# Two more places for expert weights, handed out in order of freeing, in a two-block model on one core

## The chip, the core and the metric

The kernel runs on one core of a Trainium2 chip. The metric is the device time of one execution in microseconds, the median of several runs. All data is float32; TensorE takes some operands as fp32r (a float32 written so that TensorE reads it in fewer passes). The engines are TensorE (PE), VectorE (DVE), ScalarE (ACT), GpSimd (POOL) and SyncE (SP); each works its own queue in order, and they meet by semaphores. SyncE issues nearly all weight loads.

## The reference, cut to what matters

Two blocks follow each other. The first has two layers of a hybrid mixer over 256 tokens of width 1024. The second puts 16 meta tokens ahead (272 rows in all) and has two layers, each a mixer and then a mixture of experts:

```python
def hier_moe(h, w_grp, b_grp, w_rtr, b_rtr, w1, w3, w2):
    grp_prob = softmax(t @ w_grp + b_grp)                 # 4 groups
    g_prob, g_sel = top_k(grp_prob, 1)
    exp_logits = (t @ w_rtr + b_rtr)                      # 32 experts, 8 a group
    e_prob, e_sel = top_k(softmax(in_grp), 2)             # 2 of the 8
    hid = silu(t @ w1[e]) * (t @ w3[e])                   # 1024 -> 256, for each expert e
    y = sum over e of (hid * combine[e]) @ w2[e]          # 256 -> 1024
for l in range(2):
    mix = concat(deltanet_group(...), dsa_group(...)) @ w_out[l]
    h = layer_norm(ALPHA * h + mix, ...)
    h = layer_norm(ALPHA * h + hier_moe(h, ...), ...)
```

The weights of all 32 experts are read in each of the two layers: w1 and w3 take 2 MB an expert, w2 takes 1 MB, 96 MB a layer.

## The kernel before

**The loads.** SyncE walks through one list of loads from first to last (`load`, L620 in the trace). Each load is 1 MB, 128 partitions by 2048 float32, and goes into a place ("slot") of that size. The class `Ring` works out, ahead of time, for each load its place, the count at which it has landed, and the semaphore and value that say that the last user of that place is done. SyncE waits for that value and then issues; so a load whose place isn't free holds back all loads behind it.

**The places.** Slots 0 to 5 are a ring of their own, used by all mixers in turn. In an expert stage more places are taken from tiles that are dead by then: three in `projT` (slots 6 to 8), two in the arena (`ONCE`, slots 9 and 10), one in `prm` and one more in `projT` (`LASTING`, 11 and 12). That makes 13. The list `places` starts with two ring slots, both arena slots, the three in projT, the four other ring slots, the two lasting ones; behind that a cycle of 12 repeats, the same without slot 10. SyncE waits for `delta_over` ahead of load 2 (arena is free), `room_free` ahead of load 4 (projT is free) and `layer_normed` ahead of load 11 (prm is free).

**The order of expert loads** (`moe_order`): the four "up" loads of pair 0, then for each pair its four up loads followed by the two "down" loads of the pair before. 16 pairs, 96 loads a layer. A stage is that of one layer.

**TensorE in a stage** (`experts_grouped`): `gather_pair` (L1719) picks the rows of the first pairs, `up_half(i, 0)` and `up_half(i, 1)` (L1668, 16 products of 512 columns each) wait for two loads each and count `up_used`; between them stand `turn` (L1677), `add_up` of the pair before last (L1758, adds the pair's rows into the group's sum) and small selections; then `gather_two` (L1737) and `down(i - 1)` (L1695, 16 products) on two loads. In the loads' order each of these blocks frees two places.

**ScalarE and VectorE in a stage.** ScalarE copies gathered rows (`tokens_in`, L2223), makes the sigmoid (`gate_sigmoid`, L2242 and on) and copies the high part of the down product's rows, half by half (`rows_high_out`, L2255). VectorE follows with the low part (`rows_out`, L2922). In the second half VectorE counts `down_used` once ScalarE's copy is done: that gives the two down places back (L2920).

**POOL in a stage.** It stores the normed rows to memory (L3042), gathers the rows of each of four groups by index (L3049, into `xrows`), sends the sums of the groups back by index (L3014) and reads them at the end (L3057).
**Around.** `cosT`, `sinT` (tables of the first block), `posi` (positions) and `xselT` (a selection written by ScalarE at pair 10 and read at the end of the stage) have tiles of their own. Behind the first stage comes the next layer's mixer, whose first six w_in loads go into the ring slots 3, 4, 5, 0, 1, 2.

## Time and profile before

| | us |
|---|---|
| median of 3 runs | 1416.46 |
| lowest and highest | 1414.64, 1419.3 |
| the profiled execution, its own time | 1419.17 |
| its span, first to last instruction | 1417.4 |
| TensorE busy | 1321.5 (93%) |
| VectorE busy | 572.6 (40%) |
| ScalarE busy | 487.4 (34%) |
| POOL busy | 47.2 (3%) |
| moved by the DMA engines | 306.14 MB, mean 216 GB/s |
| granted TensorE clock, mean | 0.982 |

How to read it: the first block takes the span up to about 350 us, the second block's first layer up to some 885 us with its expert stage from about 640 us on, the second layer the rest with its stage from about 1167 us on. In the view of stretches the columns are: from and to, its length, then busy us (and number of instructions) of PE, PEld (the weight loads of TensorE), DVE, ACT and POOL, the granted TensorE clock as a share, the busy share of the 16 DMA engines, and GB/s. In the chain of waits a line "issue" is time in which the engine waited for nothing that an engine or a recorded event explains; a wait for a transfer that had its landing unnoticed can stand there too. In the timeline, what stands in brackets is the idle time ahead and who ended it.

### The profile page before, as it was taken

What the parts mean: (1) busy time and instruction counts of PE and PEld (TensorE: products, weight loads), DVE (VectorE), ACT (ScalarE), POOL (GpSimd) and SP (SyncE); (2) the same over time, 40 slices, a digit from 0 to 9 for tenths busy, and PEclk for the clock granted to TensorE, in tenths of its full rate; (3) what the DMA queues carried; (4) which work ended last, traced back from release to release, by engine and by line L of the source; (5) the groups of instructions that cost most, each with busy time, mean ns of one, the idle gap of its engine ahead of it and who ended that gap; (6) DMA issues with size and microseconds to landing.
All of it is one profiled execution on the core that took longest, in us unless ns stands there. A gap on an engine that the chain in (4) does not pass through costs nothing. (4 is left out here: it accounts for less than half of the span.)

```text
span 1417.4 us, 18978 instructions
## 1 busy us (share of the span) xinstructions
PE 1321.5 (93%) x7405; PEld 845.7 (60%) x7405; DVE 572.6 (40%) x1240; ACT 487.4 (34%) x1065; POOL 47.2 (3%) x68
## 2 busy tenths in 40 slices
PE   6999989999999999989999978999998999999886
PEld 5778567784788877554344432688776654344332
DVE  2235213252577384351222214578485342222214
ACT  3245332462562234312223222473124412223222
POOL 0000000000001000000000000002000000000000
PEclk9999999999999999999999999999999999999999
DMA  8553152331521132556999999131132557999993
GB/s 343 121 148 117 60 211 89 120 119 35 208 93 58 60 126 83 208 212 237 422 420 421 422 417 381 65 110 71 60 120 90 208 215 296 420 422 422 422 423 163
DMA packets 48670, 306.14 MB, mean 216 GB/s; under 512 B 5849, under 2 KB 6361, under 8 KB 17216
## 3 DMA queue, kind: packets, MB, share of 16 engines
q1 hardware_dynamic: 43584, 285.47, 50.8%
q0 software_dynamic: 3808, 10.32, 3.0%
q10 hardware_dynamic: 1184, 9.05, 1.7%
q8 instruction: 64, 1.05, 0.3%
q14 instruction: 30, 0.25, 0.0%
HBM read 299.81 MB, written 8.59 MB: 218 GB/s over the span
## 5 line engine op out<-in xcount | busy, mean ns | idle before, releaser
L1035 PE MATMUL ps<-hT,ring 128*128 128x272 f32 (+1 forms) x1984 | 473.8, 394 | 7.0 <-ACT projT L1884 3.1
L1035 PEld LDWEIGHTS ps<-hT,ring 128*128 128x128 f32 x1984 | 375.4, 193 | 82.5 <-issue 13.3
L1668 PE MATMUL ps<-projT,arena 128*64 128x512 f32 x496 | 167.2, 596 | 7.7 <-issue 6.3
L1668 PE MATMUL ps<-ring,arena 128*64 128x512 f32 x384 | 168.1, 601 | 3.5 <-issue 3.5
L1695 PE MATMUL ps<-ring,arena 128*64 128x512 f32 x384 | 119.8, 607 | 12.3 <-issue 12.3
L1668 PEld LDWEIGHTS ps<-projT,arena 128*64 128x64 f32 x496 | 49.8, 137 | 101.1 <-issue 100.7
L2922 DVE TENSOR_TENSOR xo<-ps,xo 128x512 fp32r<-128x512 f32 x64 | 43.0, 690 | 115.4 <-ACT xo L2255 115.4
L1695 PEld LDWEIGHTS ps<-ring,arena 128*64 128x64 f32 x384 | 35.0, 138 | 78.5 <-issue 76.7
L2911 DVE TENSOR_TENSOR arena<-arena,ps 128x256 f32<-128x256 f32 x32 | 13.5, 422 | 157.7 <-ACT arena L2244 157.3
L1993 ACT ACTIVATE projT<-ps 128x272 f32<-128x272 f32 x68 | 27.0, 398 | 144.1 <-PE ps L1035 142.7
L1668 PEld LDWEIGHTS ps<-ring,arena 128*64 128x64 f32 x384 | 46.8, 137 | 32.8 <-issue 31.5
L2242 ACT ACTIVATE arena<-ps 128x256 f32<-128x256 f32 x32 | 12.3, 385 | 138.8 <-PE ps L1668 133.8
L1286 PE MATMUL ps<-ring,projT 128*128 128x512 f32 x128 | 56.6, 596 | 0.0
L2255 ACT ACTIVATE xo<-ps 128x512 fp32r<-128x512 f32 x64 | 36.7, 598 | 56.5 <-PE ps L1695 56.5
L1075 PE MATMUL ps<-ring,arena 128*128 128x512 f32 x128 | 55.9, 593 | 0.0
L1884 ACT ACTIVATE projT<-ps 128x256 f32<-128x256 f32 x56 | 21.5, 384 | 95.7 <-PE ps L1035 94.2
L1695 PE MATMUL ps<-arena 128*64 128x512 f32 x112 | 54.2, 629 | 0.0
L1668 PE MATMUL ps<-prm,arena 128*64 128x512 f32 x112 | 51.1, 598 | 0.0
L2223 ACT ACTIVATE arena<-ps 128x1024 f32<-128x1024 f32 x28 | 28.5, 1016 | 50.5 <-PE ps L1737 50.5
L2248 ACT ACTIVATE arena<-ps 128x256 f32<-128x256 f32 x32 | 12.3, 384 | 89.3 <-PE ps L1677 89.3
L1758 PE MATMUL ps<-xo,pselT 128*128 128x512 f32 x128 | 38.7, 419 | 3.0 <-DVE xo L2922 3.0
L1075 PEld LDWEIGHTS ps<-ring,arena 128*128 128x128 f32 x128 | 24.1, 190 | 28.4 <-issue 28.2
(485 smaller groups left out, 1787.4 us busy)
## 6 DMA issues: line engine op xcount, KB each, us to landing
ring<-experts SPq DMA_DIRECT2D x96, 1024.0 KB, 18.2
ring<-w_in SPq DMA_DIRECT2D x62, 1024.0 KB, 4.9
projT<-experts SPq DMA_DIRECT2D x62, 1024.0 KB, 18.3
arena<-experts SPq DMA_DIRECT2D x18, 1024.0 KB, 16.2
ring<-w_out SPq DMA_DIRECT2D x16, 1024.0 KB, 4.8
prm<-experts SPq DMA_DIRECT2D x16, 1024.0 KB, 20.9
prm<-params ACTq DMA_DIRECT2D x2, 2048.0 KB, 7.8
prm<-params ACTq DMA_DIRECT2D x2, 1152.0 KB, 10.2
```

The costliest lines, as they stand in the source:

```text
L1035: mm = pe.matmul(ps[:, 5 + j % banks, 0:ncols], w[:, j % 2, k, :], hT[:, k, T - ncols:T], start=(k == 0), stop=(k == KC - 1))
L1075: return pe.matmul(ps[:, (0, 5)[t - 1] + half, :], yT[:, 2 * GROUP_ORDER[i] + c, c0:c0 + P], w[:, c, 512 * half:512 * half + 512], start=( ...
L1286: mm = pe.matmul(ps[:, (4 if t == 1 else 2) + h, :], rows(pair, c), weights(i)[:, c, 512 * h:512 * h + 512], start=first, stop=last)
L1668: mm = pe.matmul(ps[64 * e:64 * e + 64, 0, :], xg[:, 4 * h + k, i % 2, 64 * e:64 * e + 64], w[e][:, k // 2, 512 * (k % 2):512 * (k % 2) + ...
L1695: mm = pe.matmul(ps[64 * e:64 * e + 64, 4 + half, :], xhT[:, f, 64 * e:64 * e + 64], w[e][:, f, 512 * half:512 * half + 512], start=(f == ...
L1758: mm = pe.matmul(ps[:, 6 + half, :], pselT[:, q, :], xo[:, part, 512 * half:512 * half + 512], start=(q == 0 and part == 0), stop=(q == PA ...
L1884: L(a.activation(projT[:, j, META:T], ps[:, 5 + j % 2, 0:SEQ], ACT.Copy), s("projection_copied"))
L1993: L(a.activation(projT[:, j, :], ps[:, 5 + j % 2, 0:T], ACT.Copy), s("projection_copied"))
L2223: a.activation(xg[:, 4 * half:4 * half + 4].rearrange("p (b k) c n -> p b (k c n)", b=2), ps[:, 2:4, :], ACT.Copy)\
L2255: a.activation(xo[:, 0, 512 * half:512 * half + 512], ps[:, 4 + half, :], ACT.Copy)\
L2911: VP(v.tensor_tensor(xh, xe, ps[:, 0, 0:256], ALU.mult))
L2922: v.tensor_tensor(low, ps[:, 4 + half, :], high, ALU.subtract).then_inc(s("pair_rows_copied"), 1)
```

## The change

- **Two more places.** `SPARE` (slot 13) is a new tile of 1 MB. `LENT` (slot 14) is another, in which `cosT`, `sinT`, `xselT` and `posi` now live; it is used for expert loads only up to load 57 of a stage, before `xselT` is written. The space comes from the tables that are now inside it and from the scratch of POOL's transfers, 4096 instead of 16384 bytes a partition.
- **The order.** `free` is a queue: each load takes its head and goes to its end, so places come round in the order in which their loads are used up. Ahead of a load a place whose last use is past (`LAST_USE`: LENT 57, the second arena slot 75) is dropped. The first 15 loads go to SPARE, ring, LENT, ring, both arena slots, three in projT, four ring slots, two lasting ones. Worked out, LENT is last used by load 47, the second arena slot by load 64. The waits for `delta_over`, `room_free` and `layer_normed` stand ahead of loads 4, 6 and 13.
- **ScalarE gives down weights back.** `down_used` is counted by ScalarE when TensorE's second half is done, ahead of its own copy of that half, and no longer by VectorE behind ScalarE's copy.
- **Moved.** The arena's `yacc` (used only in a branch that this input doesn't take) and `xrows` change places, so that the two arena slots stay clear; `group_tokens` gets a tile of its own. At the start two semaphores become one and one is dropped for another that counts the same instructions.

```diff
-ALL_SLOTS = 13
+SPARE, LENT = 13, 14
+ALL_SLOTS = 15
+
+LAST_USE = {LENT: 57, ONCE[1]: 75}
...
-                    rest = [*range(SLOTS, SLOTS + MORE_SLOTS), *own[2:], *LASTING]
-                    places = own[0:2] + list(ONCE) + rest
-                    cycle = own[0:2] + list(ONCE[:1]) + rest
-                    while len(places) < len(moe_order()):
-                        places += cycle
+                    free = [SPARE, own[0], LENT, own[1], *ONCE, *range(SLOTS, SLOTS + MORE_SLOTS),
+                            *own[2:], *LASTING]
+                    places = []
+                    for j in range(ITEMS_MOE):
+                        while j > LAST_USE.get(free[0], ITEMS_MOE):
+                            free.pop(0)
+                        places.append(free.pop(0))
+                        free.append(places[-1])
...
-        cosT = sb("cosT", SEQ)[:, :]
-        sinT = sb("sinT", SEQ)[:, :]
+        spare = sb("spare", SLOT)
+        lent_at = -(-nc.sbuf_base // 32) * 32
+        lent = sb("lent", SLOT)
+        assert nc.sbuf_base == lent_at + 4 * SLOT
+        cosT, sinT = lent[:, 0:SEQ], lent[:, SEQ:2 * SEQ]
+        xselT = lent[:, 2 * SEQ:2 * SEQ + T]
+        posi = nc.alloc_sbuf_tensor_at("posi", [P, SEQ], I32, offset=lent_at + 4 * (SLOT - SEQ))
+        rows_high = ctx.enter_context(nc.sbuf_tensor("rows_high", [P, D], F32R))[:, :]
...
+            if slot in (SPARE, LENT):
+                return (spare if slot == SPARE else lent)[:, :]
...
-                    if j == 2:
+                    if j == 4:
...
-                    if j == 2 + len(ONCE):
+                    if j == 6:
...
-                    if j == 2 + len(ONCE) + MORE_SLOTS + ITEMS_WO:
+                    if j == 6 + MORE_SLOTS + ITEMS_WO:
...
-        xrows, ax = more(ax, D)
         rows_low = halved("rows_low", ax, D)[:, :]
         ax += D
+        xrows, ax = more(ax, D)
...
-        group_tokens = posi[:, 0:GROUPS]
+        group_tokens = ctx.enter_context(nc.sbuf_tensor("group_tokens", [P, GROUPS], I32))[:, :]
...
                             a.wait_ge(s("pair_down_done"), 2 * i + half + 1)
+                            if half == 1:
+                                a.sem_inc(down_used, 1)
...
                         v.wait_ge(s("pair_rows_high"), 2 * i + half + 1)
-                        if half == 1:
-                            v.sem_inc(down_used, 1)
...
-    nc = bacc.Bacc("TRN2", target_bir_lowering=False, num_devices=1)
+    nc = bacc.Bacc("TRN2", target_bir_lowering=False, num_devices=1, dynamic_dma_scratch_size=4096)
```

## Rows read from the trace of the kernel before

**Rows 1.** The page's 40 equal slices: DMA busy tenths, GB/s.
```profile
DMA  8553152331521132556999999131132557999993
GB/s 343 121 148 117 60 211 89 120 119 35 208 93 58 60 126 83 208 212 237 422 420 421 422 417 381 65 110 71 60 120 90 208 215 296 420 422 422 422 423 163
```

**Rows 2.** Busy by stretch: us, busy us (instructions) per engine, PEclk, DMA, GB/s.
```profile
790.00:872.00 82.00, 70.04 (x319) 28.32 (x316) 16.64 (x27) 19.36 (x37) 2.69 (x4) 0.98 1.01 419
...
1301.00:1397.30 96.30, 83.81 (x390) 35.25 (x391) 20.36 (x37) 24.05 (x46) 3.17 (x4) 0.98 0.97 403
```

**Rows 3.** The same view, stretches of the DMA stream.
```profile
600.00:605.00 5.00, 5.00 (x13) 2.19 (x12) 3.10 (x6) 0.00 (x0) 0.00 (x0) 1.00 0.00 0
646.10:675.00 28.90, 28.27 (x148) 13.27 (x150) 7.13 (x15) 7.39 (x14) 0.00 (x0) 1.00 0.83 316
675.00:870.00 195.00, 183.73 (x876) 75.87 (x873) 45.17 (x87) 52.32 (x99) 7.77 (x9) 0.99 1.01 421
850.00:855.00 5.00, 3.83 (x11) 1.28 (x13) 0.00 (x0) 0.23 (x1) 0.00 (x0) 0.66 1.01 424
1172.60:1205.00 32.40, 31.77 (x169) 15.02 (x170) 8.35 (x19) 8.70 (x17) 1.01 (x1) 1.00 0.84 326
```

**Rows 4.** The page: POOL's DMA queue, and expert loads into the ring.
```profile
q0 software_dynamic: 3808, 10.32, 3.0%
...
ring<-experts SPq DMA_DIRECT2D x96, 1024.0 KB, 18.2
```

**Rows 5.** Chain of waits, second expert stage: start us, us, what.
```profile
1160.17 6.69 DMA arena<-normed_rows,posi
...
1184.25 3.58 PE ps L1668 x16
...
1193.69 3.58 PE ps L1668 x16
...
1198.93 3.58 PE ps L1668 x16
...
1247.81 3.58 PE ps L1668 x16
...
1373.22 3.34 issue
1376.56 5.35 PE ps L1695 x16
```

**Rows 6.** Timeline of TensorE behind the first expert stage: start us, us, what.
```profile
875.54 0.73 PE L1758 MATMUL ps<-xo,pselT 128*128 128x512 f32 x2
...
896.84 3.48 PE L1035 MATMUL ps<-hT,ring 128*128 128x272 f32 x14 [0.75 <-ACT hT L1859]
```

**Rows 7.** Timeline of SyncE's queue: start us, us over all, what, count.
```profile
646.07 0.81 SPq L620 DMA_DIRECT2D ring<-experts  x2
...
847.55 29.00 SPq L620 DMA_DIRECT2D ring<-w_in  x6
...
1172.64 0.81 SPq L620 DMA_DIRECT2D ring<-experts  x2
1177.22 0.33 SPq L620 DMA_DIRECT2D arena<-experts  x1
1183.47 4.73 SPq L620 DMA_DIRECT2D projT<-experts  x3
```

**Rows 8.** Line L620, the issues at 1172.6 and at 1208.2.
```profile
DMA to landing us min/median/max: 4.8/4.8/4.8
...
DMA to landing us min/median/max: 12.4/12.4/12.4
```

**Rows 9.** Timeline of ScalarE and VectorE: row copies of pair 0, second stage.
```profile
1194.65 1.08 ACT L2255 ACTIVATE xo<-ps 128x512 fp32r<-128x512 f32 x2
...
1195.27 1.29 DVE L2922 TENSOR_TENSOR xo<-ps,xo 128x512 fp32r<-128x512 f32 x2 [5.04 <-ACT xo L2255]
```

**Rows 10.** Line L3049, the gathers of rows: ns min/median/max.
```profile
L3049 POOL DMA_INDIRECT arena<-normed_rows,posi x8: 1009/1020/1085, 634.8 to 1310.2; - x8
```

More of the change, by code:

```diff
@@ L397, in program @@
         assert nc.sbuf_base == arena_at + 4 * AR
-        posi = ctx.enter_context(nc.sbuf_tensor("posi", [P, SEQ], I32))
-        rows_high = ctx.enter_context(nc.sbuf_tensor("rows_high", [P, D], F32R))[:, :]
         ps = ctx.enter_context(nc.psum_tensor("ps", [P, 8, 512], F32))
@@ L444, in program @@
         start_in = sem("start_in")
-        start_head = sem("start_head")
         x_in = [sem("x_in_1"), sem("x_in_2")]
@@ L458, in program @@
         rows_fetched = sem("rows_fetched")
-        seen = sem("seen")
         layer_seen = sem("layer_seen")
@@ L628, in _ @@
             head = CONSTS["few"][1]
-            sp.dma_start(cst[:, 0:head], A["consts"][:, 0:head]).then_inc(start_head, 16)
+            sp.dma_start(cst[:, 0:head], A["consts"][:, 0:head]).then_inc(start_in, 16)
             for t in (1, 2):
@@ L730, in program @@
         room = 3 * LG
-        yacc, ad = more(room, KC, T)
-        hid, ad = more(ad, 2, T)
+        hid, ad = more(room, 2, T)
         e1b, ad = more(ad, 2, T)
         cbb, ad = more(ad, T)
+        yacc, ad = more(room + 2 * D, KC, T)
         combT, ad = more(ad, T)
@@ L739, in program @@
         downw, ad = more(ad, SLOT)
+        assert ad <= AR - 2 * D
         rtmp, _ = more(ONCE_AT + len(ONCE) * SLOT, T)
@@ L1844, in _ @@
                 LT(a.activation(hT[:, k, META:T], ps[:, k % 4, 0:SEQ], ACT.Copy, scale=g_first[:, k:k + 1]), head_act)
-            a.wait_ge(seen, 1)
+            a.wait_ge(tables_vec, 16)
             L0(a.activation(sinT, sinT, ACT.Sin))
@@ L2303, in _ @@
             V0(v.memset(sg[:, 0, :], 0.0))
-            v.wait_ge(start_in, 16)
-            v.wait_ge(start_head, 16)
+            v.wait_ge(start_in, 32)
             V0(v.tensor_copy(cosT, posi[:, :]))
@@ L2316, in _ @@
             V0(v.tensor_tensor(cosT, cosT, arena[:, 4 * D:4 * D + SEQ], ALU.add))
-            V0(v.tensor_scalar(cosT, cosT, 3.1415925, -3.1415925, ALU.min, ALU.max), seen)
+            V0(v.tensor_scalar(cosT, cosT, 3.1415925, -3.1415925, ALU.min, ALU.max))
             for t in (1, 2):
```

1 line of the change is left out of this document (removed).

## The prediction

> **What bounds the kernel now.** I read the 40 slices of the page first [rows 1]. Twice, for some 200 us, the DMA line stands at 9 and the rate at 420 GB/s: those are the two expert stages, one per layer of the second block. TensorE is busy 70.0 of the last 82 us of the first stage and 83.8 of the last 96.3 us of the second [rows 2]: 12.0 and 12.5 us of waits, while before that it is busy without a break. In the chain of waits they appear as "issue" in front of L1668 and L1695, the products on expert weights, where no engine had anything left to do for them, 3.34 us the longest [rows 5]. The long stretches of the DMA engines [rows 3] show why: a stage needs 96 loads of 1 MB [rows 4], and at 421 GB/s one takes 1.0486 MB / 0.421 = 2.49 us, so the six of a pair of experts take 14.9 us. TensorE's own pace is shorter: in the chain of waits the first L1668 block of a pair stands at 1193.69 and that of the fourth pair after it at 1247.81; 54.1 us, 13.5 us a pair [rows 5]. So TensorE runs on the stock laid in before, uses it up by 790 us (1301 us in the second stage) and then follows the stream. Behind the longest wait the block takes 5.35 us and not 3.58 [rows 5]; at the same place of the first stage the granted clock is 0.66 over 5 us [rows 3], a mix of the 1.2 and the 2.4 GHz level, after an idle TensorE. The end of a stage is set by when the 94th load lands, that is by (a) how many loads are in before TensorE starts and (b) how long the DMA engines stand idle after that.
>
> As to (b): the stream opens when TensorE hands back its first places, at 646.07 us and at 1172.64 us [rows 7]. From there to 675 us it moves 316 GB/s and from 1172.6 to 1205 us 326 GB/s, against 421 afterwards [rows 3]. So 28.9 x (1 - 316/421) = 7.2 us and 32.4 x (1 - 326/421) = 7.3 us are lost in each opening. The cause is in the old order of places. The second place in the arena is used once only, so that from then on a load waits for a product later than the oldest one finished: SyncE issues one load at 1177.22 and stands till 1183.47 [rows 7].
>
> **Two more places.** 15 loads instead of 13 are in before the stage begins; 81 are left instead of 83. That is 2 x 2.49 = 5.0 us off the stream in each stage. The cost ahead: two more issues on SyncE (0.33 us for the single one [rows 7]) and 5.0 us more of transfers at about 569 and 1105 us. They are hidden: the DMA engines move nothing in 600:605 [rows 3], while all early places are full, and the loads that run beside the stores and the gather of rows at the head of the stage, four into the last ring places and two into the lasting ones, stay these six. If that cover were gone it would be up to 5.0 us a stage.
>
> **Places in order of freeing.** I walk through the second stage with SyncE's issues [rows 7] and the ends of TensorE's blocks in the chain [rows 5], two places handed back at each, 4.8 us from issue to landing on an idle queue [rows 8] and 2.49 us a load on a busy one. Returns at 1172.6, 1177.2, 1183.4, 1187.8, then at 1195.2 the down weights of pair 0 (by ScalarE, [rows 9]), then 1197.3 and 1202.5. Landings: 1177.4, 1179.9; 1182.4, 1184.9; 1188.2, 1190.7; 1193.2, 1195.7; 1200.0, 1202.5; a gather of 0.5 MB of rows by POOL comes in between, 1.2 us; 1206.2, 1208.7; 1211.2. Holes left: 0.8 us before the third pair of loads, 1.8 us before the fifth, and the first lead of 4.8 - 2.5 = 2.3 us, together 4.9 us. By bytes the opening thus loses 4.9 instead of 7.3 us, gain 2.4, with the two loads **7.4 us**. By landings it is more: the 28th load (index 27), one into the arena, was issued at 1208.2 and landed 12.4 us later, at 1220.6 [rows 8]; in my walk it lands at 1211.2, **9.4 us** earlier. Since the byte count takes every stretch between loads at the full rate and the landing count has a walk without any friction, I take the middle, 8.4 us. The first stage has the same pattern with nearly the same loss, so the same value.
>
> **ScalarE gives down weights back.** VectorE did it on its second row copy, which follows ScalarE's copy. For pair 0 ScalarE's two copies take 1194.65 to 1195.73, the second starting near 1195.2; VectorE's two differences take 1195.27 to 1196.56, the second starting near 1195.9 [rows 9]. So the hand-back comes 0.6 to 0.7 us earlier. It is of worth only where a hole stands behind it, in front of the fifth pair of loads: 0.6 us a stage, and it is already in the walk. With 81 loads that wait on the rate alone it is nothing elsewhere. The price is one semaphore instruction in ScalarE's queue ahead of the copy of the second half, 32 in all; queued behind it are that copy, VectorE's difference and the L1758 product. No row times such an instruction; the nearest is SyncE's issue of one transfer, 0.33 us [rows 7]. Only the last pair of each stage has nothing over it, and the same instruction goes from VectorE, which is next in that chain: between 2 x 0.33 us lost and 2 x 0.33 us gained. I take 0, the two being one for one.
>
> **Smaller DMA scratch.** 16384 to 4096 bytes concern POOL's transfers alone. Their queue has 3808 packets in the whole run, 238 per DMA engine [rows 4]. One of them stands on TensorE's chain at the head of each stage, the gather of rows, which took 6.69 us from issue to landing [rows 5]; the store of the rows ahead of it is of the same kind. What a smaller scratch costs no row shows. Bounds: nothing, or the landing time of the gather once more for each of the two, 13.4 us a stage. Below nothing I exclude: the transfers stay the same. I take nothing, because none of the eight gathers took over 1.085 us to issue [rows 10].
>
> The Trainium skill ("SBUF — State Buffer", SBUF size) gives the carve-out as 16 KiB, and its DMA page ("DMA: Bandwidth & Descriptors", The descriptor swizzle) counts 9 descriptors a side and engine for 1 MB; at 16 bytes each that would leave room for many such transfers in 4 KiB, which goes with nothing. No run here shows it.
>
> **The rest.** Merged start semaphores, moved tiles, a token table of its own, the swap of two row buffers: same instructions, same sizes, 0 us; the cover is not needed. The lent place leaves after load 57 and the second arena place after 75; by then loads land 18.2 us after issue in the median [rows 4] and the rate alone counts, 0 us. Behind the first stage six w_in loads are issued from 847.55 to 876.5 us, and their first product starts at 896.84 [rows 6, 7]. Now the third of them waits for the last down product; the row copies behind that one end by 875.5 us [rows 6], so it is free by 867.1 us, and 4.8 and 3 x 2.5 us more give 879.4 us, ahead of 896.84 - 8.4 = 888.4 us. 0 us.
>
> **Sum.** 2 x 8.4 = 16.8 us. What is late next: still the stream. TensorE could give back at most 12.0 + 12.5 us of waits and 2 x 1.8 us of the slow blocks, 28.1 us, so some 10 us of waits stay. The profiled execution took 1419.17 us (span 1417.4), giving 1402.4; the median of the runs shown is 2.7 us lower, 1416.46, and gives **1399.7 us**.
>
> The Trainium skill ("DMA: Bandwidth & Descriptors", Specifications) names 435 GB/s as the fabric's ceiling and about 358 GB/s as HBM's limit for a core. The trace's 421 GB/s agrees with the first and contradicts the second; by 358 a load would take 2.93 us and two of them would be worth 5.9 and not 5.0 us a stage.
>
> **The rivals.**
> Only the stock counts (chance 0.20). The holes stay, because in the opening the places come back no faster than TensorE's blocks end, whatever the order. For it: two holes remain even in my walk. Against: the one-load issue at 1177.22 goes away. 2 x 5.0 = 10 us, 1406.5, from 1404 to 1408.5.
> TensorE becomes the bound (0.07). The stream comes over 11 us earlier in each stage, if the holes left in my walk (0.8 + 1.8 us) close too. 21 to 28 us, 1388.5 to 1395.5.
> The extra stock does not stand ready, or the time is given back behind the stage (0.07): the spare loads sit in SyncE's queue behind the ring's places, and the gain melts to within 4 us. Against: nothing moves in 600:605 [rows 3], so the stock of early places is complete 40 us ahead of the stage.
> Slower (0.05): POOL's transfers wait for descriptor room. Mechanism: store and gather at the head of a stage are in TensorE's chain [rows 5]; each made longer by the gather's 6.69 us costs 13.4 us a stage, 26.8 us, less 16.8: 1426.5. It decides from 8.4 us more a stage. Against: the packets per engine above.
> The forecast has 0.58, with 1397 to 1402.5 as its own range; 0.03 lie elsewhere. A measurement of this kernel tells about 0.3%, 4.2 us, from no change. The range 1394.5 to 1407.5 takes in the forecast, most of "only the stock" and the nearer part of the TensorE case, and leaves out 0.19. Faster by more than 0.3%: 0.58 + 0.20 + 0.07 + 0.03 = 0.88; within: 0.07; slower: 0.05.
>
> **What would show it.** Right: SyncE's issues in the opening come in twos (1172.6, 1177.2, 1183.4, 1187.8), the rate from the opening on stays near 400 GB/s, TensorE's waits in the last 90 us fall from 12 to about 4 or 5 us a stage, the 3.3 us wait shrinks or goes. Wrong: the opening still at 320 GB/s (only the stock), no waits left (TensorE the bound), a longer wait before the first L1719 block (POOL), or first w_in products that wait.

## The result and the profile after

The changed kernel takes 1401.97 us in the median of four runs (1399.52 to 1404.07) and the kernel before, timed beside it, 1416.91 (1414.64 to 1419.3): ratio 0.9894, interval 0.987 to 0.9918, 14.9 us less. The profiled execution took 1402.93 us, span 1401.1. Timed once more later, the changed kernel took 1400.84 us against 1418.47: ratio 0.9874, interval 0.9854 to 0.9893. The ratios leave out two slow executions, one of 1724.14 us of the kernel with late end reads and one of 4678.78 us of the kernel before beside it. In the code everything from L620 on has moved down by eight lines or so: L620 is now L628, L1668 is L1676, L1695 is L1703, L3057 is L3064.

The DMA and GB/s lines of the page, in 40 slices, for [rows 1]:

```profile
DMA  8553252321531133556999998131132657999993
GB/s 352 117 148 110 72 214 90 121 101 50 187 119 62 61 121 120 241 207 261 419 420 421 422 417 343 68 118 63 61 120 84 277 218 289 422 421 422 421 421 141
```

The two plateaus have the same height, 421 GB/s, and the slices behind them have less left to move: 343 for 381 and 141 for 163. The megabytes in all are the same, 306.14.

The stretches, columns as in [rows 2, 3]: both openings, the last 82 and 96 us of the stages, and 5 us each around the longest wait:

```profile
641.70:670.60 28.90, 28.27 (x148) 13.30 (x150) 7.13 (x15) 7.39 (x14) 0.00 (x0) 1.00 0.95 379
776.50:858.50 82.00, 78.11 (x365) 31.11 (x365) 19.19 (x35) 21.67 (x42) 3.69 (x5) 0.98 1.01 416
842.00:847.00 5.00, 4.47 (x14) 1.79 (x16) 0.00 (x0) 0.00 (x0) 0.00 (x0) 0.66 1.02 429
1163.00:1195.40 32.40, 31.77 (x168) 14.95 (x170) 8.35 (x19) 8.69 (x17) 1.01 (x1) 1.00 0.95 371
1285.00:1381.00 96.00, 90.19 (x422) 36.53 (x418) 21.29 (x39) 26.27 (x50) 3.17 (x4) 0.96 0.95 396
1359.50:1364.50 5.00, 4.42 (x12) 1.51 (x14) 0.07 (x1) 0.60 (x1) 0.00 (x0) 0.50 1.02 428
```

The openings moved 316 and 326 GB/s before [rows 3] and move 379 and 371 now. TensorE waited 12.0 and 12.5 us at the end of a stage before [rows 2]; now 82 - 78.11 = 3.9 and 96 - 90.19 = 5.8 us.

SyncE's queue in the second opening, for [rows 7]:

```profile
1162.97 0.33 SPq L628 DMA_DIRECT2D spare<-experts  x1
1163.35 0.43 SPq L628 DMA_DIRECT2D ring<-experts  x1
1167.54 0.33 SPq L628 DMA_DIRECT2D lent<-experts  x1
1167.91 1.20 SPq L628 DMA_DIRECT2D ring<-experts  x1
1173.79 0.80 SPq L628 DMA_DIRECT2D arena<-experts  x2
```

Two loads go out at each hand-back, at 1163.0, 1167.5 and 1173.8 us, where the old order had one at 1177.22 and then stood until 1183.47 [rows 7].

The chain of waits, the longest waits of both stages and what follows them, for [rows 5]:

```profile
813.03 27.16 DMA ring<-experts
840.18 2.34 issue
842.53 5.35 PE ps L1676 x16
...
1328.91 28.78 DMA projT<-experts
1357.69 2.39 issue
1360.08 6.28 PE ps L1703 x16
```

In the chain the waits are 2.3 to 2.4 us, but in the second stage it counts as "issue" only what comes after a landing at 1357.69. TensorE's timeline has the whole idle time in brackets:

```profile
842.53 2.24 PE L1676 MATMUL ps<-ring,arena 128*64 128x512 f32 x6 [2.41 <-issue]
```

```profile
1360.08 1.09 PE L1703 MATMUL ps<-projT,arena 128*64 128x512 f32 x1 [3.71 <-issue]
```

Measured in this way, the longest wait of a stage was 3.6 and 3.3 us before, is 2.4 and 3.7 us here, and 3.9 and 3.1 us in the second execution of the changed kernel. So it has not shrunk; what went are most of the waits of about 1.2 us around it. The block behind each long wait still runs partly at the 1.2 GHz level (granted clock 0.66 and 0.50 over 5 us, in the stretches above) and takes 5.35 and 6.28 us; in TensorE's timeline a block at full clock takes 3.65.

**The length of a stage.** I take it from the start of its first up block to the start of its last down block. For the first stage these are the first of the two following lines of TensorE's timeline in the kernel before, and the second in the changed kernel, whose own first up block starts at 637.68:

```profile
641.92 4.10 PE L1668 MATMUL ps<-ring,arena 128*64 128x512 f32 x16
```

```profile
858.36 3.65 PE L1703 MATMUL ps<-ring,arena 128*64 128x512 f32 x16
```

Before, the last down block starts at 871.84 (stage 229.92 us); after, 858.37 - 637.68 = 220.69. The second stage: 1168.95 to 1397.22, 228.27 us, against 1159.27 to 1380.95, 221.68. Together 458.19 and 442.37: **15.8 us less**. All that lies outside the stages is 1417.4 - 458.19 = 959.2 us before and 1401.1 - 442.37 = 958.7 after. The part behind the last down block of the second stage, called the tail below, is 20.15 us before and 20.18 after. The other parts shift by 4 us against each other (ahead of the first stage 641.92 and 637.68, between the stages 297.1 and 300.9), while the stretches at the lower clock level lie elsewhere in each execution: the granted clock between the stages is 0.98 before and 0.96 after. The same kernel run again has 639.3 and 297.5, and 0.98 between the stages. I compare stages, therefore, and not absolute times.

### The profile page after: what moved, and what is told of

It is laid out like the page before. It is cut to its first block, busy times and chain, and to the rows that moved or that the text cites. A ratio compares the mean times of both kernels' runs of the same rounds, so it can differ in the third digit from the quotient of the medians.

```text
span 1401.1 us, 18978 instructions
## 1 busy us (share of the span) xinstructions
PE 1322.1 (94%) x7405; PEld 845.5 (60%) x7405; DVE 572.5 (41%) x1240; ACT 486.9 (35%) x1065; POOL 47.2 (3%) x68
## 2 busy tenths in 40 slices
DMA packets 48414, 306.14 MB, mean 218 GB/s; under 512 B 5849, under 2 KB 6361, under 8 KB 16704
## 4 chain that ended last, share of the span: by engine, by line
PE 76%; DVE 11%; DMA 6%; ACT 5%; issue 2%; POOL 0%; SPq 0%; DVEq 0%; ACTq 0%; POOLq 0%
PE ps L1043 24%; PE ps L1676 14%; PE ps L1703 7%; PE ps L1294 4%; PE ps L1083 4%; DMA projT<-experts 2%; PE ps L1745 2%; DMA ring<-experts 2%; PE ps L1766 2%; PE ps L1051 1%; PE ps L1513 1%; DVE projT L2578 1%; DVE small L2577 1%; PE ps L1519 1%; DMA normed_rows<-res 1%
## 5 line engine op out<-in xcount | busy, mean ns | idle before, releaser
L1043 PEld LDWEIGHTS ps<-hT,ring 128*128 128x128 f32 x1984 | 375.1, 192 | 82.4 <-issue 13.4
L1676 PE MATMUL ps<-ring,arena 128*64 128x512 f32 x416 | 140.4, 607 | 3.4 <-issue 3.4
L1676 PEld LDWEIGHTS ps<-ring,arena 128*64 128x64 f32 x416 | 40.8, 139 | 65.5 <-issue 64.5
L1676 PE MATMUL ps<-projT,arena 128*64 128x512 f32 x272 | 80.0, 597 | 0.0
L1703 PE MATMUL ps<-ring,arena 128*64 128x512 f32 x224 | 72.8, 597 | 0.0
L1703 PE MATMUL ps<-projT,arena 128*64 128x512 f32 x160 | 68.1, 615 | 4.7 <-issue 4.7
L1676 PE MATMUL ps<-arena 128*64 128x512 f32 x144 | 50.9, 597 | 1.2 <-ACT arena L2235 1.2
L1676 PE MATMUL ps<-prm,arena 128*64 128x512 f32 x96 | 43.7, 598 | 0.0
L1294 PEld LDWEIGHTS ps<-ring,projT 128*128 128x128 f32 x128 | 23.8, 190 | 28.0 <-issue 28.0
## 6 DMA issues: line engine op xcount, KB each, us to landing
ring<-experts SPq DMA_DIRECT2D x80, 1024.0 KB, 16.8
projT<-experts SPq DMA_DIRECT2D x54, 1024.0 KB, 17.6
```

Source lines behind the costliest of these rows:

```text
L1043: mm = pe.matmul(ps[:, 5 + j % banks, 0:ncols], w[:, j % 2, k, :], hT[:, k, T - ncols:T], start=(k == 0), stop=(k == KC - 1))
L1294: mm = pe.matmul(ps[:, (4 if t == 1 else 2) + h, :], rows(pair, c), weights(i)[:, c, 512 * h:512 * h + 512], start=first, stop=last)
L1676: mm = pe.matmul(ps[64 * e:64 * e + 64, 0, :], xg[:, 4 * h + k, i % 2, 64 * e:64 * e + 64], w[e][:, k // 2, 512 * (k % 2):512 * (k % 2) + ...
L1703: mm = pe.matmul(ps[64 * e:64 * e + 64, 4 + half, :], xhT[:, f, 64 * e:64 * e + 64], w[e][:, f, 512 * half:512 * half + 512], start=(f == ...
```

## The experiments

Every run below has a profile. "Stages" are the two lengths and their sum as above, "rest" is the span without them.

| kernel | stages | sum | rest | median us | ratio, interval |
|---|---|---|---|---|---|
| before | 229.92, 228.27 | 458.19 | 959.2 | 1416.91 | |
| changed | 220.69, 221.68 | 442.37 | 958.7 | 1401.97 | 0.9894, 0.987 to 0.9918 |
| changed, again | 222.91, 219.63 | 442.54 | 957.1 | 1400.84 | 0.9874, 0.9854 to 0.9893 |
| 15 places, old order | 223.45, 221.43 | 444.88 | 959.3 | 1405.56 | 0.9912, 0.9887 to 0.9937 |
| 13 places, new order | 227.17, 226.57 | 453.74 | 961.2 | 1415.4 | 0.9966, 0.9937 to 0.9996 |
| VectorE gives back | 222.81, 221.52 | 444.33 | 962.2 | 1406.34 | 0.9895, 0.9852 to 0.9937 |
| ScalarE gives back, alone | 228.80, 226.56 | 455.36 | 957.5 | 1418.58 | 1.0012, 0.999 to 1.0034 |
| small scratch, alone | 229.89, 228.30 | 458.19 | 963.0 | 1417.75 | 0.9991, 0.997 to 1.0012 |
| 14 places | 223.77, 222.79 | 446.56 | 958.6 | 1409.36 | 0.9945, 0.9923 to 0.9968 |
| half loads | 215.01, 213.39 | 428.40 | 959.4 | 1389.73 (one) | |
| late end reads | 218.10, 218.42 | 436.52 | 966.8 | 1412.22 | 0.9952, 0.9921 to 0.9984 |
| late end reads, added last | 219.02, 217.83 | 436.85 | 960.2 | 1402.18 | 0.9902, 0.9873 to 0.993 |
| reads after the last up weights | 219.07, 218.48 | 437.55 | 975.4 | 1409.99 | 0.9932, 0.9905 to 0.9958 |
| the same, added last | 218.74, 216.93 | 435.67 | 964.5 | 1404.64 | 0.99, 0.9872 to 0.9928 |

**15 places in the old order.** The fixed cycle comes back, ScalarE still gives back:

```
-                    places = []
-                    for j in range(ITEMS_MOE):
-                        while j > LAST_USE.get(free[0], ITEMS_MOE):
-                            free.pop(0)
-                        places.append(free.pop(0))
-                        free.append(places[-1])
+                    places, cycle = list(free), [x for x in free if x != ONCE[1]]
+                    while len(places) < ITEMS_MOE:
+                        places += [x for k, x in enumerate(cycle) if len(places) + k <= LAST_USE.get(x, ITEMS_MOE)]
```

> 15 places as in the changed kernel, but from load 15 on handed out in the old fixed cycle, in which the second arena place does not come again; ScalarE gives back. Theory 'stock plus order': the stock is worth 5.0 us a stage, ScalarE's hand-back 0.6; the cycle skips one place, so from load 20 on a load waits for the product after the right one, and SyncE issues a single load at the third hand-back. That keeps 2.4 us a stage of the old holes. Against the kernel before: 6 us a stage, 12 us in all, ratio 0.9915. Stage lengths (first up block to the last down block) 224 and 222 us against 229.9 and 228.3. Rival 'only the stock counts': the same time as the changed kernel, 15 us under before, ratio 0.989, stages 221 us.

Its stages are 2.5 us longer together than those of the changed kernel, near the 224 and 222 us expected. SyncE in the first opening, and the stretches of both:

```profile
656.75 0.33 SPq L625 DMA_DIRECT2D arena<-experts  x1
661.14 6.23 SPq L625 DMA_DIRECT2D projT<-experts  x3
```

```profile
645.90:674.80 28.90, 28.27 (x148) 13.32 (x150) 7.13 (x15) 7.38 (x14) 0.00 (x0) 1.00 0.88 335
1166.20:1198.60 32.40, 31.77 (x169) 15.02 (x170) 8.34 (x19) 8.69 (x17) 1.01 (x1) 1.00 0.90 352
```

The single issue is back, SyncE stands for 4 us behind it, and the rates are 335 and 352 GB/s against 379 and 371.

**13 places in order of freeing.**

```
-                    free = [SPARE, own[0], LENT, own[1], *ONCE, *range(SLOTS, SLOTS + MORE_SLOTS),
+                    free = [own[0], own[1], *ONCE, *range(SLOTS, SLOTS + MORE_SLOTS),
```

(and SyncE's three waits ahead of loads 2, 4 and 11, as before the change).

> The changed kernel with its two new places left unused: 13 places, handed out in the order of freeing, ScalarE gives back. Theory 'stock plus order': what is left is the closing of holes in the opening, 2.4 us a stage by bytes and 4.4 by landings, so 3.5 us a stage, 7 us under before, ratio 0.995; SyncE issues in twos from the first hand-back on. Rival 'only the stock counts': within 1 us of before.

The two openings:

```profile
645.80:674.70 28.90, 28.28 (x149) 13.26 (x150) 7.12 (x15) 7.38 (x14) 0.00 (x0) 1.00 0.95 355
1171.90:1204.30 32.40, 31.78 (x168) 14.92 (x170) 8.34 (x19) 8.69 (x17) 1.01 (x1) 1.00 0.96 373
```

The holes are mostly gone (DMA share 0.95 and 0.96 for 0.83 and 0.84 in [rows 3]), yet the stages are only 4.45 us shorter together, where 7 were expected. Two more places, on top of this, are worth 453.74 - 442.37 = 11.4 us.

**VectorE gives back**, as before, in an otherwise changed kernel.

```
-                            if half == 1:
-                                a.sem_inc(down_used, 1)
...
+                        if half == 1:
+                            v.sem_inc(down_used, 1)
```

> The changed kernel with one part undone: VectorE gives the down weights back behind ScalarE's copy. Theory: a load waits for it only at the fifth hand-back of each stage, 0.6 us later, so 0.6 us a stage, 1.2 us over the changed kernel (ratio to before 0.990). The issue behind the first down block comes 0.6 to 0.7 us later. Rival: ScalarE's part is worth nothing or costs something (its queue has one instruction more), then the stages are as long as in the changed kernel or shorter.

The stages are 2.1 us longer and 0.2 us shorter, one each way; the sum is 2.0 us longer, where 1.2 was expected.

**Small scratch alone**, in the kernel before: `dynamic_dma_scratch_size=4096`.

> The kernel before with the DMA scratch at 4096 bytes and nothing else. Theory: 0 us, ratio 1.000; store and gather of rows land after the same 8 and 3 to 7 us. Rival 'descriptor room': POOL's transfers in the chain ahead of each stage take longer, up to 13.4 us a stage, ratio up to 1.019.

The stages are 229.89 and 228.30 us against 229.92 and 228.27: no difference. The queue of POOL's transfers has the same packets as in [rows 4]:

```profile
q0 software_dynamic: 3808, 10.32, 2.9%
```

The ratio says the same, 0.9991 (0.997 to 1.0012).

**Half loads.** What is the floor? This kernel leaves out half of each expert load, so it shows times alone.

```
-                    load((kind, l, i, h, e), A["experts"][m * P:(m + 1) * P, :])
+                    load((kind, l, i, h, e), A["experts"][m * P:(m + 1) * P, :], 1)
...
-                                           w[e][:, k // 2, 512 * (k % 2):512 * (k % 2) + 512], ...
+                                           w[e][:, 0, 512 * (k % 2):512 * (k % 2) + 512], ...
...
-                                                w[e][:, f, 512 * half:512 * half + 512],
+                                                w[e][:, 0, 512 * half:512 * half + 512],
```

> The changed kernel, but each load of expert weights moves only its first half (0.5 MB instead of 1 MB), and TensorE reads that half in place of both. The products on expert weights thus use wrong weights, and half of the expert weights never come; the instructions of TensorE, their sizes and their order are the same. It shows how long a stage is when the stream no longer bounds it, and with that what is left to gain after the change. Theory 'the stream still sets the end of a stage': the changed kernel's stages (first up block to last down block) take 220.7 and 221.7 us; in their last 82 and 96 us TensorE waits 3.9 and 5.8 us, and about 1.8 us more are lost to one block at the lower clock level. So stages of about 215 us, no wait of over 0.5 us for a load in the chain, and a profiled time of about 1391 us (span 1389, give or take 4 us for stretches of lower clock outside the stages). Rival 'TensorE is already the bound and its own clock or VectorE and ScalarE make the waits': stages of 220 us and more, time within 3 us of 1402.

The last 82 and 96 us of its stages:

```profile
772.50:854.50 82.00, 81.33 (x393) 33.11 (x391) 19.97 (x37) 24.06 (x46) 3.69 (x5) 1.00 0.62 216
1272.00:1368.00 96.00, 95.04 (x460) 38.56 (x458) 23.81 (x43) 27.85 (x53) 4.18 (x5) 1.00 0.59 202
```

TensorE waits 0.7 and 1.0 us there, and the granted clock is 1.00. Its own work makes stages of 215.01 and 213.39 us, in all 14.0 us less than in the changed kernel and 29.8 us less than before. So the stream still sets the end of a stage after the change.

**ScalarE gives back, alone**, in the kernel before: the last edit the other way round.

> The kernel before, with one edit alone: ScalarE gives the down weights back in place of VectorE. The forecast gave 0.6 us a stage where a hole stands behind the fifth pair of loads, and nothing at the end of a stage. With it: 0 to 1.2 us less than the kernel before, 1416 us, stages of 229.3 and 227.7 us. The change without this edit had stages of 222.81 and 221.52 us against 220.69 and 221.68 with it, so a rival gives it 2 us in the first stage: 1414.5 us. Third, that it is worth something only once loads are placed in order of freeing (in the old order the load behind the hand-back waits for something later anyway): stages as in the kernel before, 229.9 and 228.3 us, within 0.3 us.

The stages are 1.1 and 1.7 us shorter, 2.8 us together; the median tells nothing (ratio 1.0012, 0.999 to 1.0034).

**14 places**, the spare one without the lent one.

> The changed kernel with one extra place instead of two (14 places: the spare one, not the lent one). By the stream's rate a place is worth one load, 2.49 us a stage. Theory 'a place is worth its bytes': between the kernel with 13 places in order of freeing (stages 227.17 and 226.57 us) and the changed kernel (220.69 and 221.68), so stages of 224 us each, whole time about 1408. Rival 'the first place does most of it, then TensorE's pace or the clock takes over': stages of 221.5 to 222.5 us, whole time about 1404. Rival 'the second does most, since only then the wait that turns the clock down is gone': stages of 226 us, whole time about 1412.

The sum, 446.56, stands between 453.74 (13 places) and 442.37 (15): 7.2 us for the first place and 4.2 for the second, 11.4 for both. The stages are near the 224 us expected of a place worth its bytes, but by this sum the first place is worth more than its 2 x 2.49 us and the second less. Why was not tried.

**The changed kernel once more.**

> The changed kernel itself once more, timed beside the one above. Both theories: 1402 us median within 3 us, ratio to the kernel before 0.986 to 0.993, stages of 221 and 222 us within 1 us. It tells how far a stage moves between executions of one kernel: if it is less than 0.5 us, the differences of 2 us between the single edits in the first stage are real; if it is 1.5 us or more, they are not.

This run put the others right. Its stages are 222.91 and 219.63 us where the first execution had 220.69 and 221.68: 2.2 us longer and 2.1 us shorter, with the same sum within 0.2. One stage of one profile can't carry a statement on 2 us, and the 2.1 us in the first stage of "VectorE gives back" are no more than that. Sums of both stages repeat far better in the two pairs on record: 442.37 and 442.54 here, 458.19 twice in the kernel before and the one with the small scratch.

**What makes one stage differ from the next.** Each load counts up its semaphore sixteen times, once by each DMA engine, and the trace has the time of each. For load 93 (counted from 0: the second down load of the last pair but one) I take the first and the last of the sixteen, both counted from SyncE's first issue of the opening. The down block of that pair waits for this load: it starts within 0.3 us of the last of the sixteen in the runs of this table, and the last down block, with which a stage ends, follows 5.8 to 6.1 us later:

| kernel | first engine, stages 1 and 2 | last engine |
|---|---|---|
| before | 212.3, 213.0 | 219.8, 218.7 |
| changed | 203.9, 205.2 | 210.6, 211.8 |
| changed, again | 204.2, 205.6 | 212.5, 209.7 |
| 15 places, old order | 206.6, 207.4 | 213.5, 211.6 |
| 13 places, new order | 209.6, 209.6 | 217.2, 216.7 |
| VectorE gives back | 207.9, 205.7 | 212.7, 211.9 |
| ScalarE gives back, alone | 212.0, 212.3 | 218.5, 216.7 |
| 14 places | 205.7, 206.7 | 213.6, 212.9 |

In the two executions of the changed kernel the first engine is done within 0.4 us of the same time. The last one, for which TensorE has to wait, is 1.9 us later in one stage and 2.1 us earlier in the other, and that is how much the stages differ. The spread from first to last is 2.0 us at load 27 and 6.7 us at load 93 of the first stage: the DMA engines drift apart while the queue is deep. With half loads, which land 4.3 and 4.7 us after issue at load 27, the spread at load 93 is 1.2 and 0.4 us. The Trainium skill ("DMA: Bandwidth & Descriptors", Why a DMA increments its semaphore by 16 and not by 1) says that the engines finish independently and that only the full 16 mean that the data is there. The trace agrees. What slows the late engine was not tried.

Between two executions of the changed kernel the first engine is the steadier measure, and by it the edits add up (mean of the two stages, us a stage): two places 209.6 - 204.6 = 5.0 in the new order and 212.2 - 207.0 = 5.2 in the old; the order 212.2 - 209.6 = 2.6 with 13 places and 207.0 - 204.6 = 2.4 with 15; ScalarE's hand-back 212.7 - 212.2 = 0.5. The 0.5 is hardly more than the 0.4 by which the measure itself moved. By the same measure VectorE's hand-back in the changed kernel costs 4.0 us in the first stage and 0.5 in the second. The second agrees with 0.5; the 4.0 stay unexplained, and the last engine is there within 0.2 us of the changed kernel's second execution (212.7 and 212.5). So the first engine too can mislead by some us.

TensorE waits for the last engine, and by that column the split is another: two places 5.8 (new order) and 5.1 (old), the order 0.7 (13 places) and 1.4 (15), ScalarE's hand-back 1.7. The lengths of the stages say the same. So the order makes most engines some 2.5 us earlier a stage and the late one, which counts, about 1. By the first engine the first extra place is worth 3.4 us and the second 1.6.

**Late end reads.** From the trace of the changed kernel: near 828 us and 1348 us POOL reads about 1.1 MB of sums back (L3064), in the middle of the last loads, though VectorE needs them only behind the last pair but one. Here POOL waits first:

```
                 g.wait_ge(sums_sent, 16 * SENT * (l + 1))
+                g.wait_ge(down_used, PAIRS * (l + 1) - 1)
```

> The changed kernel, with one wait more in POOL's queue: its three reads of the chosen rows at the end of a stage (about 1 MB, queued at some 829 us and 1349 us, in the middle of the last expert loads) wait until ScalarE has given back the down weights of the last pair but one. In the changed kernel loads 84 to 88 of the first stage land 3.7, 4.2 and 3.8 us apart instead of 2.5. Theory 'the reads take their bytes out of the stream ahead of the load that TensorE waits for': that load comes about 2.5 us earlier in each stage, the 2.4 us wait nearly goes, and with it the block at the lower clock level (1.8 us): stages of 216.5 to 219 us, whole time 4 to 8 us less than the changed kernel, 1394 to 1398 us. Rival 'the reads come too late': VectorE needs these rows for the sums that follow the stage, their landing takes 6 to 10 us, and the end of the stage waits for them: stages as in the changed kernel or shorter, but the time between the last down block and the next block's first product longer by 2 to 6 us, whole time 1400 to 1408. Third, 'hidden anyway': the load waited for is late because one DMA engine lags, not by bytes: 1402 within 1.5.

The end of the second stage in the chain of waits:

```profile
1357.48 1.38 issue
...
1362.51 1.31 issue
...
1372.38 1.27 issue
...
1378.46 4.54 DMA arena<-chosen
...
1383.02 1.24 DVE res L2944
...
1384.28 1.24 DVE res L2944
```

The wait of 3.7 us has become three of 1.3, the granted clock over the last 96 us is 1.00 for 0.96, and the stages are 5.9 us shorter together:

```profile
1283.00:1379.00 96.00, 90.92 (x438) 37.78 (x436) 21.87 (x40) 27.25 (x52) 4.15 (x5) 1.00 0.97 404
```

But behind the second stage VectorE waits 4.5 us for the reads and adds them, 2.5 us, in front of the last row difference: the tail grows from 20.18 to 23.60 us. Behind the first stage it is worse. VectorE waits 8.0 us for the reads there and TensorE 8.1 us for VectorE:

```profile
863.11 1.22 DVE L2944 SCALAR_TENSOR_TENSOR res<-res,hT 128x1024 f32<-128x1024 f32 x1 [7.97 <-DMA arena<-chosen]
```

```profile
867.62 2.07 PE L1766 MATMUL ps<-xo,pselT 128*128 128x512 f32 x4 [8.12 <-DVE xo L2929]
```

```profile
855.90:887.40 31.50, 20.80 (x78) 9.05 (x77) 19.06 (x27) 10.62 (x24) 0.06 (x1) 0.89 0.48 190
```

TensorE's clock falls behind that wait (0.89 over the stretch, 1.00 in the changed kernel). From the last down block to the first product on w_in it is 31.53 us where the changed kernel has 23.17: 8.4 us more, and with the 3.4 of the tail 11.8 us against the 5.9 gained. The rival "too late" holds.

**Late end reads, added last.** VectorE adds the rows behind its last copies:

```
-                    chosen_added(VP)
                     rows_out(PAIRS - 1)
                     sums_in(GROUPS - 1)
+                    chosen_added(VP)
```

> The kernel with late end reads, and in VectorE's queue the sum on these rows moved behind the row copy of the last pair and the copy of the last group's sums. With the late reads alone the stages were 218.10 and 218.42 us, 5.9 us less than in the changed kernel together, but what follows a stage grew from 20.18 to 23.60 us: the reads were issued at 1377.4 us, landed at 1383.0, and VectorE's row difference, with TensorE's last sums (L1766, L1803) behind it, stood behind the sum on those rows until 1385.5. Theory 'the late reads free the stream, and only the order on VectorE gave it back': stages as with the late reads alone (218.1 and 218.4); the last sums of TensorE run beside the reads and are done about 1386 instead of 1390.9 on that time scale, so 5 us less a stage than with the late reads alone: tail behind the second stage 18.5 to 19 us, whole time 1402 - 5.9 - 2 x 1.6 = about 1393 us, at most 1397. Rival 'the landing of the reads is now the bound': tail 21 to 22 us, time about 1399 to 1401, no better than the changed kernel within 0.3%.

Stages 219.02 and 217.83 (sum 436.85), tail 21.06, rest 960.2, profiled execution 1398.87 us. VectorE's queue at the end of the second stage:

```profile
1380.95 0.68 DVE L2936 COPY arena<-ps 128x512 f32<-128x512 f32 x1
1381.55 1.22 DVE L2944 SCALAR_TENSOR_TENSOR res<-res,hT 128x1024 f32<-128x1024 f32 x1
1382.80 1.22 DVE L2944 SCALAR_TENSOR_TENSOR res<-res,arena 128x1024 f32<-128x1024 f32 x1
1384.59 1.22 DVE L2727 SCALAR_TENSOR_TENSOR res<-res,ps 128x1024 f32<-128x1024 f32 x1 [0.56 <-PE ps L1803]
```

The reads are in on time here; VectorE's own two sums now stand ahead of the first sum of the norm, and the tail is 0.9 us longer. Behind the first stage VectorE still waits 1.4 us for the reads, and it is 27.00 us to the first product on w_in for 23.17. Forecast 1393, at most 1397: wrong. The median is 1402.18 us, ratio 0.9902 (0.9873 to 0.993), no better than the changed kernel beside it (0.9874).

**Reads after the last up weights**, in the two orders of VectorE: `g.wait_ge(up_used, 2 * PAIRS * (l + 1))` in place of the wait above.

> The changed kernel with POOL's three end reads held until the last up weights of the stage are given back (VectorE's order as in the changed kernel). That is about 4 us earlier than with the late end reads, which waited for the down weights of the last pair but one: issued near 1369 instead of 1374 to 1377 us, behind load 93 and into the landing of loads 94 and 95. Theory 'there is a slot for them': they land about 1376 us, VectorE adds them in its gap of 3.3 us between the row copies of the last two pairs, nothing waits for them: stages 218 to 219.5 us each (436 to 439 together, against 442.4 and 442.5 in the two executions of the changed kernel), tail 20.2 us as in the changed kernel, time 1396 to 1399 us. Rival 'a megabyte is a megabyte': they delay the last loads by 2.5 us, the last down block waits for them: stages 220 to 221 us, and the time is within 2 us of the changed kernel's 1401.

Stages 219.07 and 218.48 us (sum 437.55), tail 20.43. The stages came as the first theory had them. At the end of the second stage VectorE waited 7.5 us for the reads, as long as it had nothing else to do:

```profile
1386.27 7.48 DMA arena<-chosen
1393.77 1.24 DVE res L2944
1395.03 1.24 DVE res L2944
```

VectorE is done with them at 1396.3, just in time. Behind the first stage it was not: VectorE waited 7.1 us for the reads, TensorE 7.2 us for VectorE, and the first product on w_in came 32.18 us behind the last down block, 9.0 us later than in the changed kernel. The profiled execution took 1414.77 us, with 312.7 us between the stages where the changed kernel had 300.9 and 297.5, at a granted clock of 0.93 for 0.96 and 0.98; the median is 1409.99 us, ratio 0.9932 (0.9905 to 0.9958).

> As the other kernel of this call, with VectorE's sum on the rows moved behind the last copies too, as in the kernel with late reads added last. There the tail was 0.9 us longer than in the changed kernel (21.06 us), because VectorE's own two sums of 1.24 us stood ahead of its first sum of the norm; that stays, since it does not hang on the landing. Theory: same stages as the other kernel of this call within the scatter of 2 us a stage, tail 21.0 us, time 1 to 2 us above the other's, 1398 to 1401 us. Rival (the landing was what made the tail longer): tail 20.2 us and the two kernels equal.

Stages 218.74 and 216.93 us (sum 435.67, the shortest with whole loads), tail 21.05 us, as the theory had it, which puts the 0.9 us on VectorE's own sums. Behind the first stage it is 25.73 us to the first product on w_in. The median of 1404.64 us, ratio 0.99 (0.9872 to 0.9928), is above the 1398 to 1401 expected, and below the other order's instead of above.

All four late-read kernels have shorter stages than the changed kernel, by 4.8 to 6.7 us in sum, and none has a lower median. Their rest was up to 975.4 us (reads after the last up weights) where every kernel without late reads had 957 to 963. Part of that is the tail; the larger part that the traces show lies behind the first stage, 2.6 to 9.0 us more up to the first product on w_in. The rest differs from execution to execution with the clock. With late end reads, the four executions at a mean granted clock of 0.982 or 0.983 took 1403.32 to 1405.23 us and the six at 0.970 to 0.978 took 1412.17 to 1419.17; the changed kernel at 0.977 and 0.978 took 1401.39 to 1404.07, so the clock is not all of it. Whether the late reads bring on the lower clock elsewhere too, or just met it, is open: single executions of these kernels went down to 1396.61 us.

## Why the prediction was right

Forecast 1399.7 us, 16.8 less; measured 1401.97, 14.9 less, and 17.6 less in the second comparison. "Faster" was right, and the time is in the forecast's own range.

**What bounds the kernel**: right. With half loads the stages fall to TensorE's own pace and 0.7 and 1.0 us of waits are left.

**Two places, 5.0 us a stage by 2.49 us a load**: right; 5.0 and 5.2 by the first DMA engine, 5.7 (11.4 / 2) and 5.2 ((455.36 - 444.88) / 2) by the length of the stages. Hidden on the front side, as forecast: the rest did not grow (958.7 us for 959.2).

**Order of freeing**: the mechanism is right, SyncE's issues come in twos as in the walk. The forecast had 2.4 us by bytes and 4.4 by the walk, both with ScalarE's share, and took the middle, 3.4. Measured: 2.4 to 2.6 for the order and 0.5 for ScalarE, 3.0 us; by the length of stages the order is worth 1.3 ((444.88 - 442.37) / 2) and 0.8 us ((455.36 - 453.74) / 2), ScalarE's hand-back 1.0 and 1.4 (both sums repeat within 0.2), together 2.2 us with 13 places ((458.19 - 453.74) / 2). So the middle of 3.4 was 0.4 us too high by the first engine and 1.2 by what the stages show. The count of bytes itself came out better than forecast: by the rates of the openings 28.9 x (1 - 379/421) = 2.9 and 32.4 x (1 - 371/421) = 3.8 us are lost now, where 4.9 were expected. The landing of load 27 shows where it goes. It was to come 1211.2 - 1172.6 = 38.6 us after the first hand-back. It came at 679.8 - 641.7 = 38.1 us in the first stage, at 39.2 and 39.3 in the two stages of the second execution, and in the second stage of the first at 40.9:

```profile
DMA to landing us min/median/max: 11.0/11.0/11.0
```

That is the load issued at 1192.9 us. Fifteen of its increments had come by 1202.4, the last at 1203.9. The walk had one stream with one end; the real one has sixteen ends. Of the 9.4 us that the walk promised at this load, the first engine gained 9.0 in the mean of the four stages and the last one 8.2; at load 93 it is 7.9 and 8.1. In the opening of the kernel before the queue ran empty again and again, and a late engine could catch up. The spreads at load 27 bear this out: 1.7 to 2.4 us in all eight stages in the old order, 15 places among them, and 1.8 to 4.5 us, 3.1 in the mean, in the eighteen stages with whole loads in the new order. That the holes are what kept it small is argued from this.

**ScalarE's hand-back, 0.6 us a stage and price 0**: 0.5 us by the first engine in the kernel before, 1.4 by the length of the stages. Too small for the median to show. Nothing was lost behind the last pair: the tail is 20.15 us before and 20.18 after.

**Smaller scratch, 0 of a range from 0 to 13.4 us a stage**: right; this was the whole of the rival "slower", and it fell. The value itself was a choice: no row of before had a price for it. The Trainium skill's 16 KiB for that carve-out ("SBUF — State Buffer", SBUF size), which I could set against no row then, is a size and no need here: 4096 bytes gave the ratio 0.9991.

**The rest, 0 us**: right. The six w_in loads behind the first stage went out sooner than forecast, and TensorE's first product on them waits for ScalarE and not for a load:

```profile
847.91 16.17 SPq L628 DMA_DIRECT2D ring<-w_in  x6
```

```profile
881.53 11.27 PE L1043 MATMUL ps<-hT,ring 128*128 128x272 f32 x48 [0.75 <-ACT hT L1867]
```

**Sum.** 8.4 us a stage forecast. By the first engine of load 93 the changed kernel gained 8.4 and 7.8 us, by stage length 9.2 and 6.6, in the second execution 7.0 and 8.6; the mean of these four is 7.9 us. The mis-sized term is the order's, by some 0.4 us a stage by the first engine; by the lengths it is 1.2 too high and the places' term 0.7 too low, so that the sum came nearer than its parts. The remaining 1.1 us against the first comparison's 14.9 are within what the two comparisons differ by.

**What is late next**: "still the stream, some 10 us of waits stay" held: 3.9 + 5.8 us. "The 3.3 us wait shrinks or goes" did not: 2.4 and 3.7 us, 3.9 and 3.1 in the second execution. What the forecast did not see is why: the longest wait stands behind POOL's end reads, 1.1 MB among the last loads. With these held back it was gone.

**The rate of the stream.** The prediction says that 421 GB/s contradicts the 358 GB/s of the Trainium skill. The table there ("DMA: Bandwidth & Descriptors", Specifications) works that figure out as a memory stack's 716 GB/s divided by two cores. This kernel runs on one core, so the trace shows what one core gets and does not contradict it.

**The rivals.** "Only the stock counts" (1406.5): against it speak the first engine's 2.5 us for the order, the rates of the openings (335 and 352 GB/s in the old order, 379 and 371 in the new) and the 13 places in the new order, faster than before without any stock more (interval 0.9937 to 0.9996, ScalarE's hand-back included). It is also the nearest: 15 places in the old order with ScalarE's hand-back took 1405.56, and by the stages the order is worth only about 1 us. "TensorE becomes the bound": refuted, 14.0 us lie between the changed kernel and half loads. "Not ready, or given back": refuted, stages 15.8 us shorter and the rest 959.2 and 958.7 us. "Slower by descriptor room": refuted by the scratch alone.

## What to carry to other kernels

In a stage that ends with its stream, add up two things and nothing more: the bytes that are in before it starts, at the rate of the long plateau, and the time in which the DMA engines stand idle after it has opened. Both together, 7.4 us a stage, were here within a microsecond of what was measured (7.9), and so was the middle of 8.4; the walk from landing to landing, 9.4, was too hopeful. A place freed early is worth nothing while a queue in order stands in front of it, so hand places out in the order in which they come back; and look for other transfers in the last loads before you buy more places, but count what then waits behind them.

## What the runs showed of the hardware

A transfer is as late as its slowest DMA engine. Under a queue that never runs empty the sixteen engines drifted apart (spread at load 27 from 1.7 to 4.5 us, at load 93, some 170 us later, from 4.0 to 8.9 us in the 26 stages with whole loads), and that moved the end of a stage by 2 us between two executions of one kernel, while the first engine repeated within 0.4 us. With half loads the queue ran empty, and the spread at load 93 was 1.2 and 0.4 us.

The plateau is 419 to 422 GB/s on one core in the full slices of the changed kernel too, over the 358 GB/s that the Trainium skill gives for a core when a stack's bandwidth is divided by two ("DMA: Bandwidth & Descriptors", Specifications).

The waits of 2.4 and 3.7 us of TensorE cost 1.7 and 2.6 us more in the block behind them (5.35 and 6.28 us for 3.65), at a granted clock of 0.66 and 0.50 over 5 us. Not every wait of that length does: 3.5 us in the first stage with ScalarE's hand-back alone and 2.6 us in the second with 14 places left the block at 3.65. Three waits of 1.3 us in a row, 3.96 us together, cost nothing beyond themselves: the blocks behind them took 3.65 us and the granted clock stayed at 1.00.
